# A transformer layer on one core: router chain by token tiles, pass counts behind the first slots, identity multiplies in TensorE's waits

## The reference, cut to what matters

```
mixed = jnp.sum(gates * y, axis=2) @ w_out[l]
x = _layer_norm(DEEPNORM_ALPHA * x + mixed, ln1_g[l], ln1_b[l])
# _hier_moe: 4 groups of 4 experts, the best group, its best 2 experts
group_prob = softmax(xt @ wg_r + bg_r);  gp, gi = top_k(group_prob, 1)
exp_logits = (xt @ we_r + be_r).reshape(n_tok, N_GROUPS, EXPERTS_PER_GROUP)
top_logits, ei = top_k(exp_logits[arange, gi[:, 0]], EXPERT_TOPK)
weights = gp * softmax(top_logits)
h = silu(xt @ w_gate[e]) * (xt @ w_up[e]) * combine
y = h @ w_down[e]
```

## Time and profile before

| what | us |
|---|---|
| median of 3 runs (1378.03 to 1378.99) | 1378.92 |
| the profiled execution | 1379.11 |
| its span (first to last instruction) | 1377.4 |
| PE busy | 1318.9 (96%) |
| DVE busy | 583.0 (42%) |
| ACT busy | 483.9 (35%) |
| HBM read | 361.95 MB, 264 GB/s over the span |

### The profile page before, as it was taken

One profiled execution on the slowest core, in us unless ns is written; L12 is line 12 of the kernel. 1 busy time (PEld: TensorE's weight loads), 2 busy tenths in 40 slices (PEclk: granted clock), 3 DMA queues, 4 the chain that ended last, 5 costly groups with the idle time before them and its releaser, 6 DMA issues.

```text
span 1377.4 us, 18267 instructions
## 1 busy us (share of the span) xinstructions
PE 1318.9 (96%) x7247; PEld 965.5 (70%) x7247; DVE 583.0 (42%) x740; ACT 483.9 (35%) x659; POOL 37.1 (3%) x51
## 2 busy tenths in 40 slices
PE   7999999999999999999999999799999999999994
PEld 7989989998888888888888878554454443544431
DVE  4377445445545544554455555552122120221206
ACT  4444334335465535454333433411121120211111
POOL 0000000400000000000100000000000000000002
PEclk9999999999999999999999999899999999999997
DMA  9767555545434445555556677679999999999993
GB/s 307 230 191 250 179 187 184 184 156 167 159 130 158 142 158 183 169 168 168 188 190 232 202 244 305 243 308 421 420 422 421 422 422 422 423 422 421 422 421 153
DMA packets 116561, 364.78 MB, mean 265 GB/s; under 512 B 11480, under 2 KB 17048, under 8 KB 91168
## 3 DMA queue, kind: packets, MB, share of 16 engines
q1 hardware_dynamic: 109760, 358.79, 69.9%
q10 hardware_dynamic: 6752, 5.28, 1.3%
HBM read 361.95 MB, written 2.10 MB: 264 GB/s over the span
## 4 chain that ended last, share of the span: by engine, by line
PE 88%; DMA 6%; DVE 3%; ACT 1%; issue 1%; SPq 1%; DVEq 0%; ACTq 0%
PE main L978 19%; PE main L980 18%; PE main L979 18%; PE main L431 13%; PE att L479 6%; DMA mraw<-in_expert_w_down_dram 6%; PE att L404 4%; PE att L1217 1%; PE att L1185 1%; PE main L416 1%; PE main L417 1%; PE att L1200 1%; ACT whi L1379 1%; PE att L1236 1%; DVE wlo L1608 1%
## 5 line engine op out<-in xcount | busy, mean ns | idle before, releaser
L1608 DVE TENSOR_TENSOR wlo<-raw,whi 128x2048 fp32r<-128x2048 f32 (+1 forms) x140 | 321.8, 2299 | 371.1 <-ACT whi L1379 371.1
L1379 ACT ACTIVATE whi<-raw 128x2048 fp32r<-128x2048 f32 (+1 forms) x140 | 267.6, 1911 | 430.5 <-PE main L980 423.9
L431 PE MATMUL main<-mraw,xg 128*64 128x512 f32 x1024 | 225.0, 594 | 0.0
L978 PE MATMUL main<-whi,xhi 128*128 128x512 f32 (+1 forms) x544 | 203.9, 375 | 1.3 <-ACT uT L1418 1.3
L980 PE MATMUL main<-whi,xlo 128*128 128x512 f32 (+1 forms) x544 | 202.1, 372 | 0.0
L979 PE MATMUL main<-wlo,xhi 128*128 128x512 f32 (+1 forms) x544 | 201.9, 371 | 0.0
L431 PEld LDWEIGHTS main<-mraw,xg 128*64 128x64 f32 x1024 | 71.5, 137 | 136.2 <-issue 134.9
L978 PE MATMUL main<-xhi,whi 128*128 128x256 f32 (+1 forms) x560 | 160.2, 286 | 2.4 <-DVE wlo L1733 1.2
L979 PE MATMUL main<-xlo,whi 128*128 128x256 f32 (+1 forms) x560 | 158.9, 284 | 0.0
L980 PE MATMUL main<-xhi,wlo 128*128 128x256 f32 (+1 forms) x560 | 158.9, 284 | 0.0
L479 PE MATMUL att<-mraw,hT 128*64 128x512 f32 x512 | 113.3, 595 | 8.7 <-DMA mraw<-in_expert_w_down_dram 7.5
(11 more groups left out here) (312 smaller groups left out, 1334.5 us busy)
## 6 DMA issues: line engine op xcount, KB each, us to landing
raw<-in_w_in_dram SPq DMA_DIRECT2D x95, 1024.0 KB, 5.1
mraw<-in_expert_w_gate_dram SPq DMA_DIRECT2D x64, 1024.0 KB, 21.4
mraw<-in_expert_w_up_dram SPq DMA_DIRECT2D x64, 1024.0 KB, 23.2
mraw<-in_expert_w_down_dram SPq DMA_DIRECT2D x64, 1024.0 KB, 22.1
raw<-in_w_branch_dram SPq DMA_DIRECT2D x24, 1024.0 KB, 5.1
raw<-in_w_out_dram SPq DMA_DIRECT2D x16, 1024.0 KB, 5.3
xin<-in_x_dram SPq DMA_DIRECT2D x4, 512.0 KB, 8.0
xres<-in_x_dram SPq DMA_DIRECT2D x1, 2048.0 KB, 7.4
```

The source lines that it names most:

```text
L431: ins = pe.matmul(main[0][half, w, :], xg[:, k, half], unit[:, kk * DE:(kk + 1) * DE], start=(k == 0), stop=(k == KT - 1))
L978: pe.matmul(o, ah, bh, start=start, stop=False, skip_group_check=skip)
L1379: act.activation(whi[:, u % SPLIT, 0:n], raw[:, slot, 0:n], ACT.Copy).then_inc(hi_done, 1)
L1608: dve.tensor_tensor(wlo[:, u % SPLIT, 0:n], raw[:, slot, 0:n], whi[:, u % SPLIT, 0:n].bitcast(F32), ALU.subtract).then_inc(lo_done, 1)
```

## The change

The router's last quarter (c = 3) is handled by token tiles. The last unit multiplies all four blocks of tile 0, then those of tile 1, with a signal `rt_ok` after the first, and `route(2)` is issued between the two halves. The fold of the first three quarters (`lgT`, `fold`) is done before the last quarter; the last quarter is no longer multiplied in blocks of 32 rows but straight into the folded logits, four calls for each tile, with the transposed tile as the stationary operand. DVE, PE (transposes) and ACT (copies, 512 columns each) go tile by tile.

After the choice, PE multiplies `before` with both tiles and `ones` with tile 0 into the same bank, so that the positions need no addition afterwards; the counts come from a third call into another bank. DVE copies the positions, writes the slots of the first pair, and only then works out the pass counts. PE no longer waits for `np_ok` and `sc_free` before the first step.

`keep_warm` multiplies the identity with itself: 8 calls before the first transposes, 3 behind them, 13 after the router's logits, 3 after the position calls. Six of the expert loads signal on the semaphores of the `raw` buffers whose place they take; the values waited for are shifted by what those had counted.

```diff
+        ring = [(U1 + 10 + j - 4) % RAW if 4 <= j < 4 + RAW else None for j in range(MRAW)]
+        mlanded = [sem(f"mlanded{j}") if ring[j] is None else landed[ring[j]] for j in range(MRAW)]
+        mbase = [0 if i is None else 16 * sum(1 for u in range(1, U1 + 4 * QUADS) if u % RAW == i) for i in ring]
...
+        def keep_warm(pe, n):
+            for _ in range(n):
+                pe.matmul(att[:, 3, 0:P], ident[:], ident[:], start=True, stop=True, skip_group_check=True)
...
         def moe_pe(pe, residual_T, route):
-            residual_T(3)
-            route(3)
+            bank = main[(NCH + 2) % 2][:, 0, :]
+            lt = bank[:, 0:T * 32].rearrange("p (t n) -> p t n", t=T)[:, :, 0:NG + NE]
             pe.wait_ge(lt_out, 1)
+            pe.wait_ge(out_free, 3)
             for t in range(T):
-                ins = pe.matmul(main[0][:, 1, t * 32:t * 32 + NG + NE], lgT[:, t * P:(t + 1) * P], fold[:],
-                                start=(t == 0), stop=True, skip_group_check=True)
-            ins.then_inc(r_ps, 1)
+                pe.matmul(lt[:, t, :], lgT[:, t * P:(t + 1) * P], fold[:], start=(t == 0), stop=False,
+                          skip_group_check=True)
+            for t in range(T):
+                pe.wait_ge(out_free, 4 + t)
+                pe.wait_ge(t_out, 3)
+                for kk in range(4):
+                    k = 12 + kk
+                    ins = pe.transpose(att[:, t, kk * P:(kk + 1) * P], xr[:, t, k * P:(k + 1) * P], ident[:])
+                ins.then_inc(t_ps, 1)
+            for t in range(T):
+                pe.wait_ge(t_out, 4 + t)
+                for kk in range(4):
+                    ins = pe.matmul(lt[:, t, :], xT[:, kk, t * P:(t + 1) * P], wr[:, 12 + kk, 0:NG + NE], start=False,
+                                    stop=(kk == 3), skip_group_check=True)
+                ins.then_inc(r_ps, 1)
+            keep_warm(pe, 13)
             pe.wait_ge(sel_ok, 1)
...
-            pe.matmul(r_[:, 0:T * NE], before[:], flat, start=True, stop=True, skip_group_check=True)
-            pe.matmul(r_[:, T * NE:2 * T * NE], ones[:], flat, start=False, stop=True,
+            pe.matmul(r_[:, 0:T * NE], before[:], flat, start=True, stop=False, skip_group_check=True)
+            pe.matmul(r_[:, NE:T * NE], ones[:], sel[:, 0, :], start=False, stop=True,
                       skip_group_check=True).then_inc(pos_ps, 1)
-            pe.wait_ge(np_ok, 1)
+            pe.matmul(main[1][:, 1, 0:T * NE], ones[:], flat, start=True, stop=True).then_inc(r_ps, 1)
+            keep_warm(pe, 3)
             pe.wait_ge(z_ok, T)
...
-            pe.wait_ge(sc_free, 1)
             step(None, 0, 0)
...
         def act_tail(act, copy_T):
             copy_T(2)
+            act.wait_ge(lt_ps, 1)
+            act.activation(lgT[:], att[:, 3, 0:S], ACT.Copy).then_inc(lt_out, 1)
             act.activation(warm[:, 0:1], rowok[:], ACT.Sqrt)
-            copy_T(3)
+            for t in range(T):
+                act.wait_ge(t_ps, 4 + t)
+                act.activation(xT[:, :, t * P:(t + 1) * P], att[:, t, :].rearrange("p (k s) -> p k s", s=P),
+                               ACT.Copy).then_inc(t_out, 1)
             act.wait_ge(l1_var, 1)
             act.activation(rstd[:], bag[:, :, 1], ACT.Sqrt).then_inc(l1_std, 1)
-            act.wait_ge(lt_ps, 1)
-            act.activation(lgT[:], att[:, 3, 0:S], ACT.Copy).then_inc(lt_out, 1)
...
         def dve_moe(dve, ch):
-            dve.wait_ge(r_ps, 1)
+            dve.wait_ge(r_ps, T)
...
             dve.wait_ge(pos_ps, 1)
-            tile_n = r_[:, T * NE:2 * T * NE].rearrange("p (t e) -> p t e", t=T)
-            dve.tensor_copy(pos[:, 0, :], r_[:, 0:NE])
-            dve.tensor_copy(pos[:, 1, :], r_[:, NE:2 * NE])
-            dve.tensor_copy(tot[:], tile_n).then_inc(sc_free, 1)
-            dve.wait_ge(sc_free, 1)
-            dve.tensor_tensor(pos[:, 1, :], pos[:, 1, :], tot[:, 0, :], ALU.add)
-            link(dve.tensor_tensor(tot[:, 0, :], tot[:, 0, :], tot[:, 1, :], ALU.add))
-            link(dve.tensor_reduce(cnt[:, 0:1], tot[:, 0, :], AX.X, ALU.max))
...
-            link(dve.tensor_reduce(cnt[:, 0:1], cnt[:, 1:PASSES], AX.X, ALU.add))
...
+            link(dve.tensor_copy(pos[:].rearrange("p t e -> p (t e)"), r_[:, 0:T * NE]))
...
             slots(0, None)
+            dve.wait_ge(r_ps, T + 1)
+            dve.tensor_copy(tot[:].rearrange("p t e -> p (t e)"), main[1][:, 1, 0:T * NE]).then_inc(sc_free, 1)
+            dve.wait_ge(sc_free, 1)
+            link(dve.tensor_tensor(tot[:, 0, :], tot[:, 0, :], tot[:, 1, :], ALU.add))
+            link(dve.tensor_reduce(cnt[:, 0:1], tot[:, 0, :], AX.X, ALU.max))
...
+            link(dve.tensor_reduce(cnt[:, 0:1], cnt[:, 1:PASSES], AX.X, ALU.add))
...
                 for t in range(T):
+                    if c == 3:
+                        if t == 0:
+                            dve.wait_ge(rt_ok, 1)
+                        else:
+                            dve.wait_ge(unit_used, U1 + 4 * QUADS)
...
+                    if c == 3:
+                        ins.then_inc(out_free, 1)
+                        dve.wait_ge(out_free, 4 + t)
+                        ins = dve.bn_stats(bst[:, t, c, :], xr[:, t, cols])
...
+            keep_warm(pe, 8)
             x_transposes(range(0, 2))
+            keep_warm(pe, 3)
...
                     ins = pe.matmul(att[kk * RC:(kk + 1) * RC, 3, 0:S], wr[:, 4 * c + kk, :], xT[:, kk, :], start=(c == 0),
-                                    stop=(c == 3), skip_group_check=True)
-                if c == 3:
+                                    stop=(c == 2), skip_group_check=True)
+                if c == 2:
                     ins.then_inc(lt_ps, 1)
...
+                    last_unit = u == U1 + 4 * QUADS - 1
+                    for j in range(4 * T):
+                        kk, t = (j % 4, j // 4) if last_unit else (j // T, j % T)
...
+                        if last_unit and j == 3:
+                            ins.then_inc(rt_ok, 1)
+                            route(2)
...
-                    if n in (8, 12, 15):
-                        route((n + 1) // 4 - 2)
+                    if n in (8, 12):
+                        route(n // 4 - 2)
```

More of the change, by code:

```diff
@@ L309, in build @@
             "l1_in l1_var l1_std l1_mul z_ok acc_ok gb_in gb_ps gb_out")
-        wr_in, br_in, gw_ok, gs_ok, gs_ps, t_ps, t_out, lt_ps, lt_out, r_ps = sems(
-            "wr_in br_in gw_ok gs_ok gs_ps t_ps t_out lt_ps lt_out r_ps")
+        rt_ok, wr_in, br_in, gw_ok, gs_ok, gs_ps, t_ps, t_out, lt_ps, lt_out, r_ps = sems(
+            "rt_ok wr_in br_in gw_ok gs_ok gs_ps t_ps t_out lt_ps lt_out r_ps")
         moe_const, sel_ok, eg_in, eg_out, ed_in, ed_out, pos_ps, np_ok = sems(
             "moe_const sel_ok eg_in eg_out ed_in ed_out pos_ps np_ok")
-        mlanded = [sem(f"mlanded{j}") for j in range(MRAW)]
+        ring = [(U1 + 10 + j - 4) % RAW if 4 <= j < 4 + RAW else None for j in range(MRAW)]
+        mlanded = [sem(f"mlanded{j}") if ring[j] is None else landed[ring[j]] for j in range(MRAW)]
+        mbase = [0 if i is None else 16 * sum(1 for u in range(1, U1 + 4 * QUADS) if u % RAW == i) for i in ring]
         m_used, hot_ok, cmb_ok, xg_ps, xg_out, ws_t, wsl_out = sems("m_used hot_ok cmb_ok xg_ps xg_out ws_t wsl_out")
@@ L612, in dve_moe @@
             r_ = main[1][:, 0, :]
-            tile_n = r_[:, T * NE:2 * T * NE].rearrange("p (t e) -> p t e", t=T)
-            dve.tensor_copy(pos[:, 0, :], r_[:, 0:NE])
-            dve.tensor_copy(pos[:, 1, :], r_[:, NE:2 * NE])
-            dve.tensor_copy(tot[:], tile_n).then_inc(sc_free, 1)
-            dve.wait_ge(sc_free, 1)
-            dve.tensor_tensor(pos[:, 1, :], pos[:, 1, :], tot[:, 0, :], ALU.add)
-            link(dve.tensor_tensor(tot[:, 0, :], tot[:, 0, :], tot[:, 1, :], ALU.add))
-            link(dve.tensor_reduce(cnt[:, 0:1], tot[:, 0, :], AX.X, ALU.max))
-            for c in range(1, PASSES):
-                ins = dve.tensor_scalar(cnt[:, c:c + 1], cnt[:, 0:1], float(c * SLOTS), float(PAIRS), ALU.is_gt, ALU.mult)
-            link(ins)
-            link(dve.tensor_reduce(cnt[:, 0:1], cnt[:, 1:PASSES], AX.X, ALU.add))
-            for n, (a, b) in enumerate(((0.5, PAIRS / 2), (1.0, PAIRS), (0.5, PAIRS / 2 - 1), (1.0, PAIRS - 1))):
-                dve.tensor_scalar(runs[:, n:n + 1], cnt[:, 0:1], a, float(b), ALU.mult, ALU.add).then_inc(np_ok, 1)
+            link(dve.tensor_copy(pos[:].rearrange("p t e -> p (t e)"), r_[:, 0:T * NE]))
             def slots(pair, n):
@@ L650, in dve_moe @@
             slots(0, None)
+            dve.wait_ge(r_ps, T + 1)
[3 more added lines that the diff above has]
+            link(dve.tensor_reduce(cnt[:, 0:1], tot[:, 0, :], AX.X, ALU.max))
+            for c in range(1, PASSES):
+                ins = dve.tensor_scalar(cnt[:, c:c + 1], cnt[:, 0:1], float(c * SLOTS), float(PAIRS), ALU.is_gt, ALU.mult)
+            link(ins)
```

(25 more changed lines are left out.)

7 lines of the change are left out of this document (4 added, 3 removed).

## The result

The changed kernel takes 1370.70 us (median of 4 runs, 1370.59 to 1371.19) against 1378.95 for the kernel before (4 runs, 1378.03 to 1379.44): 8.25 us less, a ratio of 0.9942 with a 95% interval of 0.9924 to 0.9959. The profiled execution took 1371.19 us, its span is 1369.4 us.

What follows compares the result with a forecast made beforehand. PE bounds the kernel up to the router, then the expert transfers, started by the first refill; 1.8 + 2.0 + 2.3 + 1.8 = 7.9 us off 1378.92 gives 1371.0 us, range 1369.3 to 1374.0.

Steps and rivals of the forecast that it cites:

- First refill, plus a fixed 441.2 us, plus the tail: Whole expert stream: the end is set by the first refill's issue, 441.2 us to the last landing, then the tail.
- Part 1: Router's last quarter by token tiles: logits begin 1.8 us sooner, between 1.2 and 2.2.
- Part 2: From the choice to the first gather, pass counts behind the slots: 2.0 us saved, between 1.4 and 2.1.
- ahead of 889.65: Between logits and choice: the 13 identity calls run from 885.9 to 889.2, before the choice ends at 889.65.
- Part 3: Identity multiplies before the choice: the 32 gather multiplies run at the high clock, 2.3 us saved, between 0 and 2.4.
- The second rival: Router chain: the clock falls all the same, 3.8 us gained instead of 6.1, in all 1373.3; chance 0.12.
- no lower clock between the projection and the experts: Sign for the forecast: PE's clock stays high from projection to experts, with the 32 gathers in 4.0 us.
- identity multiplies ending after `sel`: Sign against the forecast: PE's identity calls behind the router's logits end later than the choice.
- Part 4: Start of the kernel: identity calls raise the clock before unit 0, 1.8 us saved, between -0.3 and 2.6.
- The first rival: Start: the clock rises no sooner, since transposes may not count as busy; no gain there, 1372.8; chance 0.17.
- Covers: Around gathers and refill: late counts charged nothing; six preloads done by 899.2, before the first refill at 899.55.
- the step from 1369.6 to 1369.3: Lower end of the range: best terms give 1369.6; with the unpriced register read it was put at 1369.3.

## Why the prediction was right

- **What sets the end.** "First refill, plus a fixed 441.2 us, plus the tail": 441.23 in the profile after, 7.99 us at the last landing for 8.00 at the refill. This reading carried the forecast. It was 441.3 to 441.6 in the profiles of six more kernels or repeats, and 442.6 and 442.9 in two others, in which the last group of loads came late (in two more the third of the last four did); so it is fixed to within about 1.7 us.
- **Part 1, router by token tiles, 1.8 us.** Measured 1.74, and 1.47 by the kernel that takes it back, where the clock was high. The terms stand: route(2) in the unit 0.64 us, DVE's residual of tile 1 at 880.08 and its transposes at 881.21, both within 0.3 us of the forecast once the start's 2.21 are added. The eight multiplies with 128-column weights for one tile took 1.0 us, by the 2.12 for both. PE's logits were expected to be the later ones, "barely", and were: the profile names DVE's `ein` as what the logits (883.91) waited for, but `ein` was done 0.35 us before, and PE's last multiply ended at 883.82. Where those multiplies took 1.92 us, at the high clock, this wait was 0.15 us.
- **Part 2, choice to first gather, 2.0 us.** Measured 1.46. This term was 0.54 too high. DVE's share was right (copy 888.63, slots 888.86, both back to back; 1.57 us came back with the counts). What failed is "ahead of 889.65": the 13 calls took 4.4 us, ran from 883.65 to 888.08 and ended 0.54 us behind the choice (887.54), since the clock was at 0.50 from 883.3 to 886.6. Where the clock did not fall (the run without the start calls) the calls ended 0.7 us ahead of the choice, and from the choice to the first gather were 2.07 us, a gain of 1.84.
- **Part 3, gathers at the high clock, 2.3 us.** Measured 2.58: 32 multiplies in a row lasted 3.75 us and not 4.0, each further one only 0.11 us. The second rival, "the clock falls in the router chain", came true for 3.4 us, at a price of 0.6 us (15.96 us from the router's multiplies to the refill, 15.38 to 15.41 in the three profiles where it did not fall: transposes, and the two without the start calls) instead of 2.3: the clock was back at 886.7, ahead of the choice, while PE ran nothing but the calls. That makes this part of the forecast right in its number and wrong in its course. Of the signs that it had named, one that was to show it right ("no lower clock between the projection and the experts") did not come, and one that was to show it wrong ("identity multiplies ending after `sel`") did.
- **Part 4, the start, 1.8 us.** Measured 2.21 to 2.27: the clock was high when unit 0 began (8.48 us), so the whole 2.1 came, and 0.2 from the faster transposes. When it rose differed from profile to profile, by the spacing of the multiplies between 4.5 us (during the eight calls) and 7.1 us (behind the transposes), but always ahead of unit 0. Whether the three calls behind the transposes are needed was not tried. ACT's second conversion now waits 1.3 us for its unit, which hides behind PE. Three runs place these 2.2 us: taking the calls away moves unit 1 back to 20.0, alone on the kernel before they bring 2.25 us, and in every profile with them unit 1 begins at 17.1 to 17.5. The first rival (transposes that don't count, so no gain) is out on both counts: the gain came, and in another place transposes held the clock.
- **Covers.** The counts are done at 891.2, gather(0) at about 892, and ACT starts its copies at 892.18: the late counts cost nothing, as charged. The six preloads were done at 896.5, 1.2 us before the refill: they fitted.
- The sum was 7.9 us. Measured 8.25 in the medians and 7.92 between the two profiled executions: +0.4 at the start, -0.5 in part 2, +0.3 in part 3. That the total is so near owes something to errors that cancel. In the range, the step from 1369.6 to 1369.3 has no term behind it: a register read could only have added time.

## What to carry to other kernels

When a stream of transfers is the bound, ask what starts it: here 5.8 us of small instructions and low clock between two phases, over 400 us from the end, came back one for one. Work that only keeps TensorE's clock up has to fill most of the wait, and its length depends on the clock itself: thirteen calls overran by 0.5 us where the clock had fallen and left 0.8 us idle where it had not, both with gathers at the high clock; ten left 1.4 us idle, the clock fell, and the gathers took 1.3 us longer. When single edits are taken back, compare them at the stage that they act on and not by the time of the whole, which here carried a surplus of up to 1.7 us from elsewhere. Before reordering multiplies, look at whether they run in pairs: an average duration taken from a busy total hides it.

## What the runs showed that was not expected

- Two float32 multiplies with 64 columns of weights each, in different halves of the array's columns, run at the same time: a step of 0.43 us for a pair, and of 0.43 us for one alone. Ordering them unit by unit made 32 of them take 8.97 us instead of 7.09.
- Transposes held the clock as well as multiplies: granted clock 1.00 and gathers in 3.76 us behind 26 transposes.
- PE's clock fell at different places in executions of the same stretch: at 883.3 us in the changed kernel, not at all with the same code behind a start that left it 2.6 us later (without the start calls; the 13 calls then took 3.15 us and ended 0.7 us ahead of the choice).
- The last groups of expert loads sometimes land 1.3 to 1.7 us late, though late and punctual executions alike moved 421 to 422 GB/s from 100 to 400 us behind the refill. What decides it was not tried.
